# Stick-breaking attention: the running sum's product as a float32r pair, and a page ring of four pairs

## The reference, cut to what matters

```python
z = einsum('bqhd,bkhd->bhqk', q, k) * HEAD_DIM ** -0.5 + bias
log_keep = where(mask, log_sigmoid(-z), 0.0)
later = cumsum(log_keep, axis=3, reverse=True) - log_keep
w = where(mask, exp(log_sigmoid(z) + later), 0.0)
out = einsum('bhqk,bkhd->bqhd', w, v)
```

## Time and profile before

| | us |
|---|---|
| median of 3 runs | 3670.58 |
| lowest, highest | 3666.86, 3671.32 |
| the profiled execution | 3670.71 |
| its span, first to last instruction | 3669.0 |
| around the span | 1.7 |
| PE busy in the span | 3335.2 (91%) |
| DVE, ACT, POOL busy | 1958.2 (53%), 1518.6 (41%), 924.4 (25%) |
| head 0's first z to the last z, start to start | 736.5 to 1722.2 |

### The profile page before, as it was taken

One profiled execution on the slowest core, in us unless ns is written; L12 is line 12 of the kernel. 1 busy time (PEld: TensorE's weight loads), 2 busy tenths in 40 slices (PEclk: granted clock), 3 DMA queues, 4 the chain that ended last, 5 costly groups with the idle time before them and its releaser, 6 DMA issues. The chain is left out here.

```text
span 3669.0 us, 47668 instructions
## 1 busy us (share of the span) xinstructions
PE 3335.2 (91%) x14713; PEld 2281.2 (62%) x14713; DVE 1958.2 (53%) x2661; ACT 1518.6 (41%) x2479; POOL 924.4 (25%) x852
## 2 busy tenths in 40 slices
PE   6987895689999999999789799999999999999998
PEld 4765673334443443443568677787778777777777
DVE  4886878888678332332435455425542555245542
ACT  3334331156655665664333244324432444223331
POOL 4994846354444333332011100000000000000000
PEclk8998996889999999999789899999999999999999
DMA  6995956287788546544455433433343333443433
GB/s 223 341 311 187 305 163 61 60 272 237 238 290 263 162 149 199 161 139 152 163 167 154 118 117 92 132 112 101 92 126 121 104 92 107 139 126 113 125 111 115
DMA packets 527265, 590.74 MB, mean 161 GB/s; under 512 B 82424, under 2 KB 338488, under 8 KB 526474
## 3 DMA queue, kind: packets, MB, share of 16 engines
q1 hardware_dynamic: 491672, 562.35, 50.0%
q10 hardware_dynamic: 35224, 25.46, 2.2%
q0 software_dynamic: 176, 0.56, 0.1%
HBM read 525.77 MB, written 61.38 MB: 160 GB/s over the span
## 5 line engine op out<-in xcount | busy, mean ns | idle before, releaser
L2371 PE MATMUL ffn_bank<-ffn_xh,ffn_wh 128*128 128x512 f32 x1408 | 557.6, 396 | 19.3 <-DVE ffn_wl L2585 18.2
L2371 PE MATMUL ffn_bank<-ffn_xl,ffn_wh 128*128 128x512 f32 x1408 | 549.4, 390 | 0.0
L2371 PE MATMUL ffn_bank<-ffn_xh,ffn_wl 128*128 128x512 f32 x1408 | 548.5, 390 | 0.0
L1423 POOL TENSOR_TENSOR att_S<-att_S,att_X 128x512 f32<-128x512 f32 (+3 forms) x256 | 314.3, 1228 | 309.5 <-PE att_bank L1674 259.6
L1563 DVE SCALAR_TENSOR_TENSOR att_X<-att_X,att_bank 128x512 f32<-128x512 f32 (+2 forms) x320 | 191.9, 606 | 341.3 <-ACT att_X L1468 340.2
L356 POOL TENSOR_TENSOR project_Kr<-project_Kr,project_q_wide 128x1024 f32<-128x1024 f32 x128 | 345.3, 2728 | 68.5 <-DMA project_Kr<-in_cache_k_dram 68.5
L2371 PEld LDWEIGHTS ffn_bank<-ffn_xh,ffn_wh 128*128 128x128 f32 x1408 | 264.8, 188 | 96.0 <-DVE ffn_wl L2585 31.1
L1669 PE MATMUL att_bank<-att_X,att_negtri 128*128 128x512 f32 (+3 forms) x640 | 294.2, 541 | 21.1 <-DVE att_X L1563 20.5
L2328 POOL TENSOR_TENSOR ffn_st<-ffn_st,kept_eps 128x1 f32<-128x1 f32 x16 | 4.9, 309 | 1216.0 <-ACT ffn_stage L2569 1119.8
L2371 PEld LDWEIGHTS ffn_bank<-ffn_xh,ffn_wl 128*128 128x128 f32 x1408 | 264.8, 188 | 56.1
L2371 PEld LDWEIGHTS ffn_bank<-ffn_xl,ffn_wh 128*128 128x128 f32 x1408 | 265.0, 188 | 52.2
(11 more groups left out here) (362 smaller groups left out, 6299.9 us busy)
## 6 DMA issues: line engine op xcount, KB each, us to landing
att_Vr<-in_cache_v_dram SPq DMA_DIRECT2D x512, 256.0 KB, 3.6
project_Kr<-in_cache_k_dram SPq DMA_DIRECT2D x320, 256.0 KB, 4.3
ffn_wdf<-in_w_down_dram SPq DMA_DIRECT2D x108, 512.0 KB, 3.3
att_Kr<-in_cache_k_dram SPq DMA_DIRECT2D x192, 256.0 KB, 3.7
ffn_stage<-in_w_gate_dram SPq DMA_DIRECT2D x89, 512.0 KB, 3.8
ffn_stage<-in_w_up_dram SPq DMA_DIRECT2D x88, 512.0 KB, 4.5
project_w<-in_w_in_dram SPq DMA_DIRECT2D x40, 512.0 KB, 6.3
project_xt<-in_x_prompt_dram SPq DMA_DIRECT2D x16, 512.0 KB
```

What stands on the lines that cost most here:

```text
L1423: pool.tensor_tensor(new[:, r:], old[:, r:], x[:, r:], ALU.add).then_inc(s_part, 1)
L2371: mm = pe.matmul(bank[:, first + f % 2, :], w[:, j, k, :], x[:, k, :], start=(k == 0 and n == 0), stop=(k == KD - 1 and n == 2))
```

## The change

`S` gets three slots. After POOL has made the running sum, ACT rounds it to float32r (`Sh`), and DVE subtracts that from the sum to give the rest (`Sl`, float32r, two inputs from SBUF). PE's product by the running sum becomes two float32r products, with `Sh` and with `Sl`. The mask's product becomes float32r too. ACT does the rounding of unit s - 2 in step s, between Ln and the weights' exp; DVE does the rest of unit s - 3 in step s, behind the softplus and ahead of the page work. Units with j = 0 have no sum (36 of 40 have one). POOL's sum no longer waits for PE: it waits for `sl_ready` of the unit three before, for its softplus, and for its own last sum. ACT rounds three constant 128 x 128 tiles once. The ring `Kr` of the attention is four pairs of pages in place of six; that of the projection stays.

```diff
+KL = 4
-        NX, NW, NZ = 4, 4, 5
+        NX, NW, NZ, NSUM = 4, 4, 5, 3
-        S = m.sb("S", [P, 2, CH])
+        S = m.sb("S", [P, NSUM, CH])
+        Sh, Sl = m.sb("Sh", [P, NSUM, CH], F32R), m.sb("Sl", [P, NSUM, CH], F32R)
+        ones_r, ident_r, fill_r = (m.sb(n, [P, P], F32R) for n in ("ones_r", "ident_r", "fill_r"))
-        Kr = m.sb("Kr", [P, KR, PP, AW])
+        Kr = m.sb("Kr", [P, KL, PP, AW])
...
-                        old, new = S[:, (u - 1) % 2, :], S[:, u % 2, :]
-                        pool.wait_ge(logw_ready, b * NU + u)
+                        old, new = S[:, (u - 1) % NSUM, :], S[:, u % NSUM, :]
+                        if u >= NSUM:
+                            v = max(v for v in range(u - NSUM + 1) if carries(v))
+                            pool.wait_ge(sl_ready, b * CARRIES[-1] + CARRIES[v])
+                        else:
+                            pool.wait_ge(sl_ready, b * CARRIES[-1])
                         pool.wait_ge(sp_ready, b * NU + u + 1)
+                        if u:
+                            pool.wait_ge(s_part, b * SUMS[-1] + SUMS[u - 1])
...
+                def round_carry(b, u):
+                    o = cols(u)
+                    act.wait_ge(s_part, b * SUMS[-1] + SUMS[u])
+                    if not (isinstance(b, int) and b == 0 and u < NSUM):
+                        act.wait_ge(logw_ready, b * NU + u - NSUM + 2)
+                    act.activation(Sh[:, u % NSUM, o:], S[:, u % NSUM, o:], ACT.Copy).then_inc(sh_ready, 1)
...
                             act.activation(x, x, ACT.Ln, bias=1.0).then_inc(l_ready, 1)
+                        r, u = behind(b, s, 2, first, rest)
+                        if u is not None and carries(u):
+                            round_carry(r, u)
...
+                        def rest_of_carry():
+                            r, u = behind(b, s, 3, first, rest)
+                            if u is None or not carries(u):
+                                return
+                            o = cols(u)
+                            dve.wait_ge(sh_ready, r * CARRIES[-1] + CARRIES[u])
+                            tt(Sl[:, u % NSUM, o:], S[:, u % NSUM, o:], Sh[:, u % NSUM, o:].bitcast(F32), ALU.subtract).then_inc(sl_ready, 1)
...
                             softplus()
+                        rest_of_carry()
...
-                                    pe.matmul(bank[:, s % NZ, o:o + P], ident[:], fillm[:], start=False, stop=False,
+                                    pe.matmul(bank[:, s % NZ, o:o + P], ident_r[:], fill_r[:], start=False, stop=False,
...
-                                pe.wait_ge(s_part, r * SUMS[-1] + SUMS[u - 1])
-                                last = pe.matmul(bank[:, u % NZ, o2:], negones[:], S[:, (u - 1) % 2, o2:], start=False, stop=True,
-                                                 skip_group_check=True)
+                                pe.wait_ge(sl_ready, r * CARRIES[-1] + CARRIES[u - 1])
+                                for part in (Sh, Sl):
+                                    last = pe.matmul(bank[:, u % NZ, o2:], ones_r[:], part[:, (u - 1) % NSUM, o2:], start=False, stop=False,
+                                              skip_group_check=True)
```

More of the change, by code:

```diff
@@ L1189, in stage_attention @@
     SUMS = [sum(steps(v) for v in range(u + 1)) for u in range(NU)]
+    carries = lambda u: U[u][1] != 0
+    CARRIES = [sum(carries(v) for v in range(u + 1)) for u in range(NU)]
     with ExitStack() as ctx:
@@ L1235, in stage_attention @@
         z_ready, e_ready, l_ready, sp_ready = (m.sem(n) for n in ("z_ready", "e_ready", "l_ready", "sp_ready"))
-        s_part, s_sum, logw_ready, w_ready, av_done = (m.sem(n) for n in ("s_part", "s_sum", "logw_ready", "w_ready", "av_done"))
+        s_part, logw_ready, w_ready, av_done = (m.sem(n) for n in ("s_part", "logw_ready", "w_ready", "av_done"))
+        sh_ready, sl_ready = m.sem("sh_ready"), m.sem("sl_ready")
+        rounded = m.sem("rounded")
         odd_copied, o_copied, o_stored = m.sem("odd_copied"), m.sem("o_copied"), m.sems("o_stored", 2)
@@ L1331, in load_k @@
                         skip_runtime_bounds_check_because="DVE has put every id of the table between 0 and the last page")
-                    if kk >= KR:
-                        sp.wait_ge(k_summed, kk - KR + 1)
+                    if kk >= KL:
+                        sp.wait_ge(k_summed, kk - KL + 1)
                     for k, page in enumerate(ids[::-1]):
-                        sp.dma_start(Kr[:, kk % KR, k, :], cache_k[bass.ds(page, 1)].rearrange("o s c -> s (o c)")).then_inc(k_loaded[kk % KR], 16)
+                        sp.dma_start(Kr[:, kk % KL, k, :], cache_k[bass.ds(page, 1)].rearrange("o s c -> s (o c)")).then_inc(k_loaded[kk % KL], 16)
                 for i in range(LATE):
@@ L1339, in _ @@
                 sp.wait_ge(table_ready, 1)
-                for kk in range(KR):
+                for kk in range(KL):
                     load_k(kk)
@@ L1450, in split @@
                     act.activation(qlb[HD:P, cs], wide[HD:P, :], ACT.Copy, scale=bias_now[HD:P, :]).then_inc(b_filled, 1)
+                act.wait_ge(consts, 8)
+                for out, src in ((ones_r, negones), (ident_r, ident), (fill_r, fillm)):
+                    act.activation(out[:], src[:], ACT.Copy).then_inc(rounded, 1)
                 for c in (3, 2):
                     split(0, c)
+                def round_carry(b, u):
[4 more added lines that the diff above has]
+                    act.activation(Sh[:, u % NSUM, o:], S[:, u % NSUM, o:], ACT.Copy).then_inc(sh_ready, 1)
                 def round_(b, steps, first, last, rest):
@@ L1584, in round_ @@
                             seq, n = late_pair(kk)
-                            page = Kr[:, kk % KR]
+                            page = Kr[:, kk % KL]
                             if kk == 0:
                                 dve.wait_ge(q_loaded, 16 * LATE)
-                            dve.wait_ge(k_loaded[kk % KR], 16 * PP * (kk // KR + 1))
+                            dve.wait_ge(k_loaded[kk % KL], 16 * PP * (kk // KL + 1))
                             tt(page, page, q_late[:, seq, None, :].to_broadcast([P, PP, AW]), ALU.mult).then_inc(k_used, 1)
@@ L1620, in _ @@
                 pe.wait_ge(consts, 8)
+                pe.wait_ge(rounded, 3)
                 def samples_v(b, n):
```

10 lines of the change are left out of this document (4 added, 6 removed).

## The result

The change makes the kernel slower: 3736.91 us in the median of 4 runs (3726.61 to 3740.01), against 3669.84 for the kernel before on the same chip (4 runs, 3666.86 to 3671.32). The ratio is 1.0188, 95% interval 1.0174 to 1.0202. The profiled execution took 3726.61 us, its span is 3724.9. Forecast were 3719, in a range of 3650 to 3750.

A forecast was written before the change was run, and what follows sets the result against it. DVE's queue was taken to bound the page stretches of heads 0 to 3, PE heads 4 to 7. 4 x (25.6 - 2.5) - 44 = +48 us on 3670.7 gives 3719 us, range 3650 to 3750.

The forecast's parts named there:

- DVE full in the stretches, and POOL between rest and multiply: Page work of heads 0 to 3: POOL's sum delays DVE's multiply, steps 2.98 to 4.66 us, +25.6 us a stretch.
- The first rival: Page stretches: POOL does not get between rest and multiply, stretches grow only 8.7 us, 3652 us in all; chance 0.2.
- PE's product: Two float32r products for one float32 save 0.38 us per 512 columns, 11.4 us a head; masks about 1.0 more.
- Heads 4 to 7, 44 us: Heads where PE sets the pace: each gains 11 us, 44 us in all.
- DVE's part, where PE sets the pace: nothing: Heads 4 to 7: a 0.68 us subtraction a step costs nothing, DVE being idle two thirds of the time.
- the 1.4 that I took for ACT: ACT's added rounding, thinly covered in steps 33 to 39, takes 1.4 us a head off PE's gain; ends 0 and 4.
- Outside the stretches in heads 0 to 3: Rest of heads 0 to 3, beyond their page work: PE gains 3.7 us, gives back 1.2, net 2.5 a head.
- The ring, "costs nothing": Four page pairs suffice at 4.66 us a step; at 3.6 DVE would wait up to 2 us a head.
- The clock as a rival: Page stretches: PE, less busy, drops to 1.2 GHz; a third of steps so costs 40 us, 3760; chance 0.1.

The follow-up runs named there:

- Experiment 1: The changed kernel with DVE's rest moved behind the page sum in the steps with page work; 3701.13 us, ratio 1.0081 to the kernel before.
- experiment 6: The changed kernel with POOL's running sum again also waiting for PE's use of the last sum; 3707.07 us, ratio 1.0114 to the kernel before.
- experiment 4: The changed kernel with the rest's subtraction replaced by an equally long DVE reduce with one SBUF input; 3717.1 us, ratio 1.0124 to the kernel before.
- Experiment 2: The changed kernel without DVE's subtraction, PE adding the product by the rounded sum twice; 3636.29 us, ratio 0.99 to the kernel before.
- experiment 5: The changed kernel with ACT's rounding put behind the weights' exp; 3725.82 us, ratio 1.0156 to the kernel before.
- experiment 7: The changed kernel with the float32r pair in heads 4 to 7 alone, heads 0 to 4 written out; 3635.57 us, ratio 0.9911 to the kernel before.

## Why the prediction was right, point by point

**DVE full in the stretches, and POOL between rest and multiply:** right, mechanism and size. The forecast was 4.66 us a step, 25.6 a stretch, a mean multiply of 1.9 and stretches near 100; measured 4.67, 25.8, 1.88 and 100.5 on average. Experiment 1 removes the 1.06 us by order alone, and experiment 6 by POOL's time alone. The first rival, in which the multiply follows the rest at once, needed a multiply of 1.25 and is out.

In all these runs the order is that in which the two engines come, not the place in DVE's queue: POOL came 0.24 us into the rest and ran before a multiply that DVE had next in line. The rule of the Trainium skill, "SBUF — State Buffer", "Who interferes with whom", names a GpSimd instruction that reads SBUF beside a two-input one of DVE. The trace agrees on who blocks whom: POOL's sum takes 1.58 us behind the two-input rest and 1.28 behind or beside a one-input instruction (experiments 4 and 6). The page's "issue order" must be read across the engines.

**PE's product:** right. 0.40 us a full step against 0.38, and the mask saves 0.11 to 0.13 each where I had 0.05 to 0.1.

**Heads 4 to 7, 44 us:** a mis-sized term. They gain 33.0, that is 8.3 a head and not 11. The step that failed is "DVE's part, where PE sets the pace: nothing". Experiment 2, without the rest, gains 10.2 a head, so the rest costs 2.0 where I had nothing. The other 3.1 (12.4 and 0.9 more for the masks as measured, less 10.2) stand against the 1.4 that I took for ACT; moving ACT's rounding (experiment 5) did not bring them back. Part of them stands where the loop of rounds turns back: from a head's second z to its third it is 3.7 to 3.9 us before and 4.3 to 4.5 after in heads 4 to 6, but 2.3 and 2.0 in head 7, which has no such turn and gains 10.4. What else is in them stays open. I had argued with DVE's share of idle time, but the rest is on PE's path at a head's start, where DVE splits q and k. From DVE's timeline in head 6, and what PE waited for:

```profile
1573.75 0.68 DVE L1569 TENSOR_TENSOR att_qlb<-att_qf,att_qhh 64x512 fp32r<-64x512 f32 x1 [3.30 <-ACT att_kh L1458]
1574.46 0.69 DVE L1570 TENSOR_TENSOR att_khl<-att_kf,att_khl 64x512 fp32r<-64x512 f32 x1
1575.18 0.56 DVE L1588 SCALAR_TENSOR_TENSOR att_X<-att_X,att_bank 128x384 f32<-128x384 f32 x1
1575.66 0.28 DVE L1596 TENSOR_TENSOR att_Sl<-att_S,att_Sh 128x128 fp32r<-128x128 f32 x1
```

```profile
1575.99 0.33 PE L1709 MATMUL att_bank<-att_Sh,att_ones_r 128*128 128x128 f32 x1 [1.12 <-DVE att_Sl L1596]
```

DVE first waits 3.30 us for ACT's split, with the rest behind it, and PE 1.12 for the rest. From 1342 to 1690 us, most of head 4, all of 5 and 6 and the start of 7, PE and its weight loads waited for the rest 7 and 17 times (9.3 and 18.1 us). I had named ACT alone as the suspect if these heads gained under 8 us. Three gain 7.1 to 7.9, and DVE's rest is 2.0 a head of what is missing, on average.

**Outside the stretches in heads 0 to 3:** a gain of 2.5 us a head was forecast. Heads 0 to 3 lose 101.8 in all and their stretches 103.3, so it is 0.4 a head. The 9 us missing here and the 11 of heads 4 to 7 are why the attention lost 68.8 and not 48. In the profiled execution the stages outside the attention took some 13 us less than in the one of before, with the same code; head 0's first z lies between 729 and 738 us over all these profiles. That is in part why its 3726.61 came so close to 3719, and the median of 3736.91 is 18 above it.

**The ring, "costs nothing":** right for this kernel (no wait but head 0's first), and for the reason given. The other half of that step was that at 3.6 us a step DVE would wait up to 2 us a head. Two kernels have such steps. In experiment 1 it is 3.3 to 4.2 us in each of heads 1 to 3, which is more; in experiment 6 it is 0.9 to 2.5, about as said. In both, head 0 has no wait behind its first. The 2.02 us above stand behind a narrow softplus, where a step is shorter than the 3.6 us that I reckoned with.

**The clock as a rival:** its sign is there, its price is not. The granted clock in the stretches fell to 0.78, 0.98, 0.93 and 0.96, but they last 99.8, 100.8, 100.6 and 100.7 us: the stretch's length does not follow the clock. PE is idle for 25 us or more in each, and DVE is full throughout.

## What to carry to other kernels

An engine's share of idle time is no cover for an instruction that another engine waits for: ask in each stage what stands ahead of it in its queue. Where DVE and POOL both read SBUF, what counts is which instruction of DVE is running when POOL's comes. Let it be one with one SBUF input, or let POOL come while the long one already runs, and put no short instruction just ahead of the long one where POOL is released while the short one runs. A trade of PE time for DVE time should be made only in the heads in which PE sets the pace; here experiment 7, which does so, is 0.9% faster than the kernel before, and by the estimate above about two thirds of that is left without what else it changes.

## What the runs showed that I had not expected

- A wait can be worth having. POOL's wait for PE looked like a mere constraint; putting it back (experiment 6) takes some 30 us off, because it moved POOL's sum away from DVE's multiply.
- A DVE instruction with one SBUF input does not hold POOL up (1.28 us in experiment 4, against 1.58 behind a two-input one), and still lets POOL in ahead of a multiply that follows it.
- A unit's mask product in float32r saves 0.11 to 0.13 us, in most steps from 0.14 to 0.06 start to start.
- ACT stands idle for 2.2 to 2.6 us where the loop of rounds turns back, as long in both kernels, and a head without that turn is 3.0 to 3.1 us shorter (heads 4 and 5 of experiment 7).
